# ScalarE does its part of an expert step behind the next block's first tile; the steps are dealt out anew; TensorE adds even slots' rows from slot 184

## The chip, the core and the metric

One core of a Trainium2 chip runs the whole program. The metric is the device time of one execution in microseconds (us), lower is better. The core has TensorE (PE, its weight loads are PEld), VectorE (DVE), ScalarE (ACT), GpSimd (POOL) and SyncE (SP), each with its own instruction queue; they wait for each other by semaphores, and 16 DMA engines move data for all of them. "Granted clock" is the share of full speed at which TensorE was allowed to run (1.0 is 2.4 GHz, 0.5 is 1.2 GHz).

## What is computed

Two transformer blocks over 512 positions of width 1024, all in float32. The first has chunked attention with a learned bias, a gated short convolution and a squared-ReLU feed-forward part. The second mixes stick-breaking attention and an mLSTM, and ends in a mixture of single-vector experts, which is where most bytes are read:

```python
def peer(h, w_q, sub_keys, expert_u, expert_v):
    q = einsum('bsd,dq->bsq', h, w_q)                       # 8 heads x 2 halves of 128
    scores = einsum('bshpc,hpnc->bshpn', q, sub_keys)
    top_s, top_i = lax.top_k(scores, 16)                    # per half
    cand_s, cand_i = all 256 sums and index pairs
    best_s, best_pos = lax.top_k(cand_s, 16)
    gate = softmax(best_s)                                  # 8 heads x 16 = 128 experts a token
    ...
    u = jnp.take(expert_u, ib, axis=0)                      # a row of 1024 per token and expert
    act = gelu(einsum('td,tkd->tk', xb, u))
    vv = jnp.take(expert_v, ib, axis=0)
    return einsum('tk,tkd->td', gate * act, vv)
```

## The kernel before, in words

The 512 positions are cut into two halves of 256 (`hf` 0 and 1), and each half goes through both blocks. A half is a list `SEQ` of weight **blocks**: Q1, K1, V1, CG, XC, BG, then attention with GC, CP and GA worked in between its items, then AP, WO, 16 UP, 16 DN (the feed-forward part), then for the second layer QKM, Q2, K2, V2, VM and OM (worked in between the stick-breaking heads), the mLSTM without blocks, WO2 and 8 PQ. A block is 1 MB of weights (256 columns, into a ring of four buffers by SyncE) and two **tiles** of 8 matmuls each (lines 496 and 499, two records a matmul), whose results ScalarE or VectorE take out of PSUM. There are four PSUM lanes, so TensorE can be four tiles ahead.

The experts of half 0 are worked off beside the blocks of half 1. 512 **slots** stand for them: a slot is one expert for each of 128 tokens, 128 slots to a tile of tokens. GpSimd gathers a slot's 128 rows of u and v together, 1 MB (line 449). Slots come in groups, of two up to slot 255 and of four after it. An **expert step** is the work of VectorE and ScalarE on one group, and each engine has it as a generator, `expert_steps`, which `tick` calls once after every block of half 1 but six, and the stick-breaking loop once more for every even head (`next(experts_act)`, `next(experts_dve)`). I number steps so that step k takes the dot products of group k and finishes group k-1:

- VectorE's step k: `coef` of group k-1 from ScalarE's GELU of it (line 1241, it waits for `gelu_done`), one weighted addition into `acc` for each slot (line 1256), then two dot products of group k (line 1229). Every eighth step also picks 16 more experts, the **routing** (lines 1184 to 1211).
- ScalarE's step k: it waits for VectorE's dot products of group k and does their GELU (line 888).
- From `FIRST_PE` = slot 208 on, an even slot's v row is added by TensorE instead of by VectorE: ScalarE makes a diagonal matrix of the coefficient (line 881), TensorE multiplies (line 477).

So VectorE's step k needs ScalarE's step k-1, and ScalarE's step k needs VectorE's step k. There are six gather buffers until slot 208, so up to that slot the gathers follow VectorE's pace. From 208 on (`CHANGE`, in GpSimd's list) the weight ring and other memory are free and there are 16 buffers. 100 of the steps lie beside blocks; the others follow when the last block is done.

Order is what is written: each engine's program is generated in the order of the text. Other lines that the prediction speaks of: the stick-breaking loop runs over 8 heads c. VectorE subtracts the sums (1609), adds the softplus of the next head (1597), takes in the logits of the one after (1593), and does its step at the end of the position. ScalarE does an exponential (1087), the three of `soft` for head c+2 (1077, 1079, 1081), takes out a tile of VM or OM (1094), and does its step. TensorE does logits (638), sums (648, 652), a VM or OM tile (496, 499) and values (664). In PQ, TensorE has a tile, then `side_scores` (830); ScalarE takes out the tile (1144) and the scores (1133); VectorE searches the 16 best of each score list (1690 to 1698, "top-k"). Then come transposes (850) and copies (1160), for which VectorE waits. Sums of squares for a norm are lines 912 (ScalarE) and 520 (TensorE), for heads 927 and 534.

Of the kernel before, what the change touches and what calls it, by code (L numbers as in the profile page):

```python
# [111 lines left out]

FIRST_PE = 208

# [25 lines left out]

TICKS = [int(hf == 1 and (kind, i) not in ((BG, 3), (WO, 3), (DN, 15), (V2, 0), (V2, 1), (WO2, 3))) for hf, kind, i in SEQ]
EARLY = sum(TICKS) + 4 > GROUP_OF[15 * TOPK]


def build(nc, a, out):
    ctx = ExitStack()
    with ctx:
# [314 lines left out]
        def _(pe):  # L462
# [20 lines left out]

            def weights_block(n, moving, token_major=False, first=True, last=True, fresh=None, single=False):

                pe.wait_ge(w_loaded[n % NRING], 16 * (n // NRING + 1))
                for t in range(2):
# [15 lines left out]
                    mm.then_inc(tile_done, 1)  # L503
                    if t == 0 and n:
                        for _ in range(TICKS[n - 1]):
                            next(experts_pe)
                    yield t

# [221 lines left out]
            def half(hf):  # L730
# [104 lines left out]
                for i in range(8):  # L835
                    for _ in weights_block(NO[hf, PQ, i], h, fresh=KT * (4 * hf + 3) if i == 0 else None):
                        if m:
                            side_scores(m - 1)
                        m += 1
                side_scores(15)  # L840
                pe.wait_ge(sc_done, 16 * (hf + 1))
# [29 lines left out]
        def _(act):  # L871
# [27 lines left out]
            ticked = []  # L899

            def tick(hf, kind, i):
                n = NO[hf, kind, i]
                ticked.append(n)
                for _ in range(TICKS[n]):
                    next(experts_act)

# [11 lines left out]
            def head_squares(hf, kind, m0, raw, root=None):  # L918

                for i in range(COUNT[kind]):  # L920
                    n = NO[hf, kind, i]
                    for t in range(2):
                        m = m0 + 2 * i + t
                        tile_wait(act, n, t)
                        if m >= 4:
                            act.wait_ge(ms_done, m - 3)
                        act.activation(scr[:, m % 4, :], out_tile(n, t), ACT.Square).then_inc(sq_done, 1)
                        act.activation(raw[:, 2 * i + t, :], out_tile(n, t), ACT.Copy).then_inc(evac_sem(n, t), 1)
                        if root is not None and 2 * i + t == 0:
                            head_root(hf, root)  # L930
                    tick(hf, kind, i)
# [8 lines left out]
            def evacuate(hf, kind, dst, func=ACT.Copy, root=None, **kw):  # L940

                for i in range(COUNT[kind]):
                    n = NO[hf, kind, i]
                    for t in range(2):
                        j = 2 * i + t
                        tile_wait(act, n, t)
                        extra = {k: v(j) for k, v in kw.items()}
                        act.activation(dst(i, t), out_tile(n, t), func, **extra).then_inc(evac_sem(n, t), 1)
                        if root is not None and j == 0:
                            head_root(hf, root)  # L950
# [7 lines left out]
            def attention(hf):  # L958
# [34 lines left out]

                def fill_ticks(tiles):
                    for j in tiles:
                        if j % 2:
                            tick(hf, FILL1[j // 8], j % 8 // 2)

                act.wait_ge(ms_done, 32 * hf + 16)
                exps(0)  # L1000
                for i in range(N_ITEMS + 1):
# [6 lines left out]
                    if i >= 2:  # L1008
                        prob_copy(i - 2)
                    fill_ticks(filled(i - 1))  # L1010
                prob_copy(N_ITEMS - 1)
                fill_ticks(filled(N_ITEMS))

            def half(hf):
# [17 lines left out]
                for i in range(16):  # L1032
                    n = NO[hf, UP, i]
                    for t in range(2):
# [3 lines left out]
                        evac_wait(act, n, t)  # L1038
                        act.activation(u, u, ACT.Square).then_inc(relu_sq, 1)
                    tick(hf, UP, i)  # L1040
                only_ticks(hf, DN)
# [6 lines left out]
                for j in range(8):  # L1048
# [5 lines left out]
                    if t:  # L1054
                        tick(hf, QKM, j // 2)
                tanh_half(7)
                head_squares(hf, Q2, 32 * hf + 16, QS)
# [7 lines left out]
                act.wait_ge(gate_act, 3 * hf + 2)  # L1065
                act.activation(row_a, row_a, ACT.Ln, bias=ones_1[0:NML, 0:1]).then_inc(gate_act, 1)

                _, zb, ab = sb_bufs(hf)
# [16 lines left out]
                for c in range(NH2):  # L1085
# [11 lines left out]
                    elif hf:  # L1097
                        next(experts_act)
                for j in range(4):
# [39 lines left out]
                for m in range(16):  # L1139
# [7 lines left out]
                    if t:  # L1147
                        tick(hf, PQ, m // 2)
                    if (hf, m) == (0, 7):
                        gate_exps(0)  # L1150
# [15 lines left out]
            half(1)  # L1166
            assert ticked == [n for n in range(NB) if SEQ[n][1] != ADA]
            if EARLY:
                gate_exps(16)
# [5 lines left out]
        def _(dve):  # L1175
# [161 lines left out]
            def attention(hf):  # L1337
# [39 lines left out]
                for i in range(N_ITEMS + 1):  # L1377
# [8 lines left out]
                    for j in filled(i):  # L1386
                        if j % 2:
                            tick(hf, FILL1[j // 8], j % 8 // 2)
                y_copy(7)

            def half(hf):
# [193 lines left out]

                only_ticks(hf, V2)
                dve.wait_ge(neg_done, 5 * hf + 3)
# [193 lines left out]
```

## Time and profile before

| | |
|---|---|
| median of 3 runs | 2891.6 us (2891.0 to 2894.65) |
| the profiled execution, its own time | 2893.74 us |
| its span in the profile | 2892.0 us |
| TensorE matmul, VectorE, ScalarE, GpSimd busy | 79%, 63%, 22%, 27% |
| mean granted clock | 0.888 |
| read from HBM | 790 MB, 275 GB/s over the span |

Half 0 ends and half 1 begins at 959 us. The last block ends at 2056 us; after that only the experts are left. The busy shares are means over stages with different limits, so the stages are read one by one.

### The profile page before, as it was taken

How to read it: one execution, taken by the hardware profiler on the slowest of the kernel's cores; microseconds unless marked ns; L12 is line 12 of the kernel's file. 1: busy time of each engine (PE TensorE's matmuls, PEld its weight loads, DVE VectorE, ACT ScalarE, POOL GpSimd, SP SyncE). 2: the span in 40 equal slices, each digit the busy share in tenths (PEclk: the TensorE clock that was granted, in tenths of full speed). 3: DMA queues.
4: the chain of work that ended last, by engine and by line, in shares of the span. 5: the costliest groups of instructions: out<-in, count | busy, mean ns of one | idle time of the engine just before them, and what ended most of it. 6: DMA issues, size and time to landing. Idle time of an engine off the chain costs nothing. (4 is left out here: it accounts for less than half of the span.)

```text
span 2892.0 us, 26202 instructions
## 1 busy us (share of the span) xinstructions
PE 2280.8 (79%) x9012; PEld 1681.2 (58%) x9012; DVE 1826.5 (63%) x3679; ACT 647.0 (22%) x1438; POOL 776.5 (27%) x544
## 2 busy tenths in 40 slices
PE   8999999989889998899899689987444555445554
PEld 6887788878668777677788566766311221112121
DVE  1122235413237679667777785758888888888886
ACT  1103212002611310462221115621111111111110
POOL 0000000000000244223443331312375545546552
PEclk9999999999979999899999888998677877777777
DMA  4343357643124699677899873634599999999996
GB/s 161 120 149 117 122 188 289 260 149 121 69 102 185 249 348 415 215 271 291 363 421 421 366 297 120 253 143 192 200 406 421 411 421 422 421 402 422 422 421 276
DMA packets 114660, 798.24 MB, mean 276 GB/s; under 512 B 13280, under 2 KB 16480, under 8 KB 19040
## 3 DMA queue, kind: packets, MB, share of 16 engines
q0 software_dynamic: 74880, 541.10, 46.3%
q1 hardware_dynamic: 39648, 255.47, 23.7%
q8 instruction: 72, 1.18, 0.2%
q14 instruction: 60, 0.49, 0.0%
HBM read 790.23 MB, written 6.29 MB: 275 GB/s over the span
## 5 line engine op out<-in xcount | busy, mean ns | idle before, releaser
L499 PE MATMUL PS<-reg,ring 128*128 128x256 f32 x6016 | 1381.0, 388 | 34.0 <-DVE reg L1324 13.5
L499 PEld LDWEIGHTS PS<-reg,ring 128*128 128x128 f32 x6016 | 1149.2, 194 | 221.6 <-issue 52.1
L449 POOL DMA_INDIRECT uv<-in_expert_uv,experts x322 | 519.7, 1614 | 1927.3 <-DVE experts L1211 915.1
L477 PE MATMUL PS<-uv,diag 128*128 128x512 f32 x228 | 154.2, 828 | 239.7 <-ACT diag L881 239.7
L1256 DVE SCALAR_TENSOR_TENSOR acc<-uv,coef,acc 128x1024 f32<-128x1024 f32 x261 | 335.3, 1285 | 10.3 <-DVE coef L1241 1.1
L1229 DVE CUSTOM_DVE_ANT_0 uv<-uv,h_tok 128x1024 f32<-128x1024 f32 x226 | 268.9, 1219 | 41.6 <-DMA uv<-in_expert_uv,experts 41.3
L477 PEld LDWEIGHTS PS<-uv,diag 128*128 128x128 f32 x228 | 59.1, 274 | 339.4 <-issue 339.4
L888 ACT ACTIVATE acts<-dots 128x2 f32<-128x2 f32 (+1 forms) x192 | 39.1, 204 | 944.9 <-DVE dots L1229 896.1
L477 PE MATMUL PS<-reg,diag 128*128 128x512 f32 x228 | 156.7, 840 | 103.9 <-ACT diag L881 103.9
L477 PEld LDWEIGHTS PS<-reg,diag 128*128 128x128 f32 x228 | 58.2, 270 | 200.0 <-issue 200.0
L449 POOL DMA_INDIRECT reg<-in_expert_uv,experts x114 | 141.2, 1238 | 88.7 <-PE PS L477 62.7
L1229 DVE CUSTOM_DVE_ANT_0 uv<-uv,reg 128x1024 f32<-128x1024 f32 x96 | 116.5, 1225 | 58.3 <-DMA uv<-in_expert_uv,experts 58.3
L477 PE MATMUL PS<-ring,diag 128*128 128x512 f32 x152 | 89.1, 726 | 61.9 <-ACT diag L881 61.9
L496 PE MATMUL PS<-ring,reg 128*128 128x256 f32 x512 | 117.3, 384 | 0.0
L449 POOL DMA_INDIRECT ring<-in_expert_uv,experts x76 | 106.3, 1399 | 33.6 <-issue 20.4
L1229 DVE CUSTOM_DVE_ANT_0 reg<-reg 128x1024 f32<-128x1024 f32 x96 | 112.8, 1220 | 3.4 <-DMA reg<-in_expert_uv,experts 3.4
L496 PEld LDWEIGHTS PS<-ring,reg 128*128 128x128 f32 x512 | 95.8, 191 | 18.5 <-issue 6.4
L477 PEld LDWEIGHTS PS<-ring,diag 128*128 128x128 f32 x152 | 31.8, 223 | 112.0 <-issue 112.0
L1334 DVE SCALAR_TENSOR_TENSOR reg<-reg,par,PS 128x256 f32<-128x256 f32 x64 | 28.4, 477 | 97.6 <-PE PS L552 97.6
L888 ACT ACT_TABLE_LOAD x52 | 66.7, 1283 | 98.2 <-issue 56.5
L1347 DVE SCALAR_TENSOR_TENSOR reg<-PS,toep 128x128 f32<-128x128 f32 (+1 forms) x64 | 31.2, 488 | 90.6 <-PE PS L584 86.0
L1476 DVE SCALAR_TENSOR_TENSOR tmp<-ring,silu_c,tmp 128x256 f32<-128x256 f32 x168 | 81.4, 485 | 6.0
(240 smaller groups left out, 2314.1 us busy)
## 6 DMA issues: line engine op xcount, KB each, us to landing
ring<-in_weights SPq DMA_DIRECT2D x228, 1024.0 KB, 6.8
uv<-in_expert_uv,experts POOLq DMA_INDIRECT x322
reg<-in_x_t SPq DMA_DIRECT2D x2, 1024.0 KB, 5.9
kv_half<-reg SPq DMA_DIRECT2D x1, 2048.0 KB, 10.7
reg<-in_sub_t SPq DMA_DIRECT2D x2, 1024.0 KB, 4.8
toep<-in_rel_pad SPq DMA_DIRECT2D x16, 128.0 KB, 5.1
x_tokens<-reg SPq DMA_DIRECT2D x2, 1024.0 KB, 9.1
reg<-kv_half SPq DMA_DIRECT2D x1, 2048.0 KB, 14.3
```

The lines of the kernel that those rows point to most:

```text
L449: gp.indirect_dma_start(UV[r], None, a["expert_uv_2"], bass.IndirectOffsetOnAxis(ap=experts[:, e % 256:e % 256 + 1], axis=0))\
L477: mm = pe.matmul(PS[:, 6 + j, :], diag[:, n % 4, :], UV[BUF[s]][:, D + 512 * j:D + 512 * j + 512], start=begins, stop=ends, **LAX)
L496: mm = pe.matmul(out_tile(n, t), mv[:, t * P:(t + 1) * P], w, start=first and k == 0, stop=last and k == KT - 1)
L499: mm = pe.matmul(out_tile(n, t), w[:, t * P:(t + 1) * P], mv, start=first and k == 0, stop=last and k == KT - 1)
L888: act.activation(acts[:, s0 % 16:s0 % 16 + s1 - s0], dots[:, s0 % 16:s0 % 16 + s1 - s0], ACT.Gelu)\
L1229: dve.tensor_tensor_reduce(out=u, in0=u, in1=H2[s // 256][:, s // NSLOT % 2, :], scale=1.0, scalar=0.0, op0=ALU.mult, op1=ALU.add, accum_o ...
L1256: dve.scalar_tensor_tensor(acc[:, :], v, c, acc[:, :], ALU.mult, ALU.add).then_inc(acc_done, 1)
L1334: dve.scalar_tensor_tensor(tile, tile, gain, PS[:, b, c0:c0 + T], ALU.mult, ALU.mult).then_inc(hn_done, 1)
L1347: dve.scalar_tensor_tensor(PROB[:, i % 4, 0:w], PS[:, i % 3, 0:w], HD1 ** -0.5, toep[:, hd % 2, w - 1::-1], ALU.mult, ALU.add).then_inc(s_ ...
L1476: dve.scalar_tensor_tensor(ac, ring[:, n % NRING, k, :], silu_c[:, k:k + 1], ac, ALU.mult, ALU.add)\
```

## The change

1. `ScalarE's` step is postponed. `tick` no longer does it but owes it (`owe`), and `settle` does it after the first tile of the next block has been taken out. In the list `SEQ` positions where only ticks stand, a tick settles the one before. In the stick-breaking loop `next(experts_act)` becomes `owe(1)`, and no `settle` stands inside the loop.
2. Steps are dealt out anew (`NO_STEP`, `MORE`). No step any more after BG 1, DN 11, DN 13, DN 14, QKM 1, QKM 3; new ones after V2 0 and V2 1, and three inside attention, after the first tiles of three of its blocks. That is 99 steps beside blocks where there were 100. VectorE's two V2 steps stand among the head scalings.
3. `FIRST_PE` is 184: even slots 184 to 206, 12 in all, are now TensorE's. In PQ, TensorE's part stands behind `side_scores`.

```diff
-FIRST_PE = 208
+FIRST_PE = 184
...
-TICKS = [int(hf == 1 and (kind, i) not in ((BG, 3), (WO, 3), (DN, 15), (V2, 0), (V2, 1), (WO2, 3))) for hf, kind, i in SEQ]
+NO_STEP = ((BG, 1), (BG, 3), (WO, 3), (DN, 11), (DN, 13), (DN, 14), (DN, 15), (QKM, 1), (QKM, 3), (WO2, 3))
+MORE = (2, 10, 18)
+TICKS = [int(hf == 1 and (kind, i) not in NO_STEP) for hf, kind, i in SEQ]
...
-                for _ in weights_block(NO[hf, PQ, i], h, fresh=KT * (4 * hf + 3) if i == 0 else None):
+                    n = NO[hf, PQ, i]
+                    for t in weights_block(n, h, fresh=KT * (4 * hf + 3) if i == 0 else None, steps=False):
                         if m:
                             side_scores(m - 1)
                         m += 1
+                        if t == 0:
+                            for _ in range(TICKS[n - 1]):
+                                next(experts_pe)
...
+            def settle():
+                for _ in range(owed[0]):
+                    next(experts_act)
+                owed[0] = 0
+            def owe(steps):
+                settle()
+                owed[0] = steps
             def tick(hf, kind, i):
                 n = NO[hf, kind, i]
                 ticked.append(n)
-                for _ in range(TICKS[n]):
-                    next(experts_act)
+                owe(TICKS[n])
...
                         act.activation(raw[:, 2 * i + t, :], out_tile(n, t), ACT.Copy).then_inc(evac_sem(n, t), 1)
+                        if t == 0:
+                            settle()
...
                     for j in tiles:
                         if j % 2:
                             tick(hf, FILL1[j // 8], j % 8 // 2)
+                        elif hf and j in MORE:
+                            owe(1)
+                        settle()
...
                 act.activation(row_a, row_a, ACT.Ln, bias=ones_1[0:NML, 0:1]).then_inc(gate_act, 1)
+                settle()
...
                     if t:
                         tick(hf, kind, i)
                     elif hf:
-                        next(experts_act)
+                        owe(1)
...
+                tick(hf, V2, 0)
                 for m in range(8):
                     head_scale(hf, 2, m, (QS if m < 4 else KS)[:, m % 4, :], col("q_g_2" if m < 4 else "k_g_2"))
+                    if m == 3:
+                        tick(hf, V2, 1)
...
-                only_ticks(hf, V2)
```

**The stick-breaking loop, ScalarE, half 1.** From the tile of head 0 (line 1094) on, through head 1. The 128x896 operations are one head's; `acts<-dots` is the step's GELU. Before:

```order
L1094 ACTIVATE reg<-PS 128x256
L888 ACT_TABLE_LOAD
L888 ACTIVATE acts<-dots 128x2
L1087 ACT_TABLE_LOAD
L1087 ACTIVATE reg<-reg 128x896
L1077 ACTIVATE reg<-reg 128x896
L1079 ACTIVATE reg<-reg 128x896
L1081 ACT_TABLE_LOAD
L1081 ACTIVATE reg<-reg,ones 128x896
L1094 ACTIVATE reg<-PS 128x256
L888 ACT_TABLE_LOAD
L888 ACTIVATE acts<-dots 128x2
```

After, the same place (the tile is line 1134, the GELU line 905):

```order
L1134 ACTIVATE reg<-PS 128x256
L1127 ACT_TABLE_LOAD
L1127 ACTIVATE reg<-reg 128x896
L1117 ACTIVATE reg<-reg 128x896
L1119 ACTIVATE reg<-reg 128x896
L1121 ACT_TABLE_LOAD
L1121 ACTIVATE reg<-reg,ones 128x896
L1134 ACTIVATE reg<-PS 128x256
L905 ACT_TABLE_LOAD
L905 ACTIVATE acts<-dots 128x2
```

The GELU behind head 0's tile is gone, and one stands behind head 1's tile: it is head 0's.

**The PQ blocks, half 1, late ones.** ScalarE before, from the first tile of a block (1144 a tile, 1133 scores) over its step to the next block's tile:

```order
L1144 ACTIVATE reg<-PS 128x256
L1133 ACTIVATE reg<-PS 128x2x128
L1144 ACTIVATE reg<-PS 128x256
L1133 ACTIVATE reg<-PS 128x2x128
L888 ACTIVATE acts<-dots 128x2
L1144 ACTIVATE reg<-PS 128x256
```

ScalarE after, from the first tile of a block on (1184, 1173; 898 is the diagonal, 905 the GELU):

```order
L1184 ACTIVATE reg<-PS 128x256
L1173 ACTIVATE reg<-PS 128x2x128
L898 ACTIVATE diag<-ident,coef 128x128
L905 ACTIVATE acts<-dots 128x2
L1184 ACTIVATE reg<-PS 128x256
L1173 ACTIVATE reg<-PS 128x2x128
L1184 ACTIVATE reg<-PS 128x256
```

TensorE at the same place, before and then after (830 and 843 are `side_scores`, 488 is the addition of an expert's row):

```order
L830 MATMUL PS<-reg 128x128 x2
L499 MATMUL PS<-reg,ring 128x256 x8
L830 MATMUL PS<-reg 128x128 x2
L499 MATMUL PS<-reg,ring 128x256 x8
L830 MATMUL PS<-reg 128x128 x2
```

```order
L843 MATMUL PS<-reg 128x128 x2
L488 MATMUL PS<-uv,diag 128x512 x2
L510 MATMUL PS<-reg,ring 128x256 x8
L843 MATMUL PS<-reg 128x128 x2
L510 MATMUL PS<-reg,ring 128x256 x8
L843 MATMUL PS<-reg 128x128 x2
```

The step moved from behind a block's second tile to behind the next block's first tile and scores, and TensorE has an addition ahead of each second tile from the fourth block on.

**Head scaling after V2, VectorE, half 1.** Before, from the inverse of the root on:

```order
L1329 RECIPROCAL hroot<-hroot 128x256
L1546 MEMSET reg 128x896
L1550 COPY reg<-strict 128x128 x2
L1334 SCALAR_TENSOR_TENSOR reg<-reg,par,PS 128x256 x8
L1556 TENSOR_SCALAR toep<-PS,par 4x256 x2
```

After (1377 is the scaling; 1284, 1299, 1272 are a step's coefficient, additions and dot products):

```order
L1372 RECIPROCAL hroot<-hroot 128x256
L1591 MEMSET reg 128x896
L1595 COPY reg<-strict 128x128 x2
L1284 TENSOR_TENSOR coef<-acts,gates 128x2
L1299 SCALAR_TENSOR_TENSOR acc<-uv,coef,acc 128x1024 x2
L1272 ISA uv,dots<-uv,h_tok 128x1024
L1272 ISA dots 128x1
L1272 ISA uv,dots<-uv,h_tok 128x1024
L1272 ISA dots 128x1
L1377 SCALAR_TENSOR_TENSOR reg<-reg,par,PS 128x256 x4
L1284 TENSOR_TENSOR coef<-acts,gates 128x2
L1299 SCALAR_TENSOR_TENSOR acc<-uv,coef,acc 128x1024 x2
```

Two steps stand now among the eight scalings, one before and one after the first four.

## Rows read from the trace of the kernel before

**Rows 1.** Table by stretch; the first row names its columns.

```profile
core 0: us, PE busy (x) PEld busy (x) DVE busy (x) ACT busy (x) POOL busy (x), PEclk, DMA share, GB/s
1167.00:1335.00 168.00, 160.16 (x740) 117.39 (x740) 116.35 (x230) 93.69 (x182) 44.35 (x24) 0.98 0.69 241
1407.00:1630.00 223.00, 223.00 (x1022) 195.79 (x1022) 166.85 (x266) 39.56 (x105) 88.36 (x59) 0.99 0.98 403
...
1791.00:1858.00 67.00, 66.37 (x330) 53.78 (x328) 54.44 (x74) 48.91 (x54) 26.04 (x14) 1.00 0.67 251
1954.00:2070.00 116.00, 76.72 (x320) 63.29 (x319) 97.50 (x328) 15.42 (x45) 29.43 (x16) 0.83 0.45 169
2103.00:2892.00 789.00, 395.54 (x608) 149.15 (x608) 672.14 (x1181) 123.83 (x312) 403.95 (x306) 0.75 0.98 405
```

**Rows 2.** Page: an addition. Line engine op, tiles, shapes, count | busy, mean ns | idle.

```profile
L1256 DVE SCALAR_TENSOR_TENSOR acc<-uv,coef,acc 128x1024 f32<-128x1024 f32 x261 | 335.3, 1285 | 10.3 <-DVE coef L1241 1.1
```

**Rows 3.** Timeline, TensorE after DN, half 0 and 1: start, us, what [idle before <-releaser].

```profile
642.72 3.62 PE L520 MATMUL PS<-scr,ones_d 128*128 128x256 f32 x16
...
1651.10 5.51 PE L520 MATMUL PS<-scr,ones_d 128*128 128x256 f32 x16 [20.57 <-ACT scr L912]
```

**Rows 4.** Timeline, TensorE, first head mean of Q2, half 1.

```profile
1710.33 1.12 PE L534 MATMUL PS<-scr,half_sel 128*64 128x256 f32 x2 [13.19 <-ACT scr L927]
```

**Rows 5.** Timeline, VectorE, second pair of head scalings after V2, half 1.

```profile
1756.31 0.87 DVE L1334 SCALAR_TENSOR_TENSOR reg<-reg,par,PS 128x256 f32<-128x256 f32 x2 [3.83 <-PE PS L552]
```

**Rows 6.** Timeline, all engines, one position of the stick-breaking loop.

```profile
1801.01 0.12 DVE L1241 TENSOR_TENSOR coef<-acts,gates 128x2 f32<-128x2 f32 x1
...
1805.98 1.08 DVE L1609 TENSOR_TENSOR reg<-reg,PS 128x896 f32<-128x896 f32 x1
1806.13 1.28 ACT L888 ACT_TABLE_LOAD   x1 [0.62 <-DVE dots L1229]
...
1806.98 1.08 DVE L1597 SCALAR_TENSOR_TENSOR reg<-reg 128x896 f32<-128x896 f32 x1
...
1808.39 0.70 PE L648 MATMUL PS<-reg,tri 128*128 128x256 f32 x2
...
1811.34 0.14 DVE L1241 TENSOR_TENSOR coef<-acts,gates 128x2 f32<-128x2 f32 x1
...
1811.97 3.62 PE L496 MATMUL PS<-ring,reg 128*128 128x256 f32 x16
...
1815.63 0.38 ACT L1094 ACTIVATE reg<-PS 128x256 f32<-128x256 f32 x1 [0.22 <-PE PS L496]
```

**Rows 7.** Timeline, the loop's end: a GELU without a wait, the mLSTM's start.

```profile
1847.54 1.28 ACT L888 ACT_TABLE_LOAD   x1
...
1848.83 0.20 ACT L888 ACTIVATE acts<-dots 128x2 f32<-128x2 f32 x1
...
1869.86 1.19 PE L695 MATMUL PS<-toep,ident 4*128 4x256 f32 x2 [6.08 <-DVE reg L1601]
```

**Rows 8.** Timeline, VectorE and TensorE in PQ.

```profile
2001.24 6.14 PE L499 MATMUL PS<-reg,ring 128*128 128x256 f32 x16
...
2007.31 0.14 DVE L1241 TENSOR_TENSOR coef<-acts,gates 128x2 f32<-128x2 f32 x1
...
2013.25 0.29 DVE L1690 MAX8 reg<-reg 128x8 f32<-128x128 f32 x1 [0.86 <-ACT reg L1133]
...
2020.09 0.14 DVE L1241 TENSOR_TENSOR coef<-acts,gates 128x2 f32<-128x2 f32 x1
```

**Rows 9.** Timeline, between the last block and the last stretch.

```profile
2077.44 0.16 DVE L1241 TENSOR_TENSOR coef<-acts,gates 128x2 f32<-128x2 f32 x1 [3.69 <-ACT reg L1160]
...
2082.85 0.16 DVE L1241 TENSOR_TENSOR coef<-acts,gates 128x2 f32<-128x2 f32 x1 [0.32 <-ACT acts L888]
...
2115.87 0.40 ACT L881 ACTIVATE diag<-ident,coef 128x128 f32<-128x128 f32 x1 [0.23 <-DVE coef L1241]
...
2116.42 1.95 PE L477 MATMUL PS<-uv,diag 128*128 128x512 f32 x4 [0.68 <-ACT diag L881]
```

More of the change, by code:

```diff
@@ L139, with fill_tile_no @@
     _held[_r] = _e
-TICKS = [int(hf == 1 and (kind, i) not in ((BG, 3), (WO, 3), (DN, 15), (V2, 0), (V2, 1), (WO2, 3))) for hf, kind, i in SEQ]
-EARLY = sum(TICKS) + 4 > GROUP_OF[15 * TOPK]
+NO_STEP = ((BG, 1), (BG, 3), (WO, 3), (DN, 11), (DN, 13), (DN, 14), (DN, 15), (QKM, 1), (QKM, 3), (WO2, 3))
+MORE = (2, 10, 18)
+TICKS = [int(hf == 1 and (kind, i) not in NO_STEP) for hf, kind, i in SEQ]
+STEPS = sum(TICKS) + 4 + len(MORE)
+EARLY = STEPS > GROUP_OF[15 * TOPK]
+def fill_tile_no(n, t):
+    _, kind, i = SEQ[n]
+    return 8 * FILL1.index(kind) + 2 * i + t
 def build(nc, a, out):
@@ L482, in _, with weights_block @@
             experts_pe = expert_steps()
-            def weights_block(n, moving, token_major=False, first=True, last=True, fresh=None, single=False):
+            def weights_block(n, moving, token_major=False, first=True, last=True, fresh=None, single=False, steps=True):
                 pe.wait_ge(w_loaded[n % NRING], 16 * (n // NRING + 1))
@@ L503, in weights_block @@
                     mm.then_inc(tile_done, 1)
-                    if t == 0 and n:
+                    if t == 0 and n and steps:
                         for _ in range(TICKS[n - 1]):
                             next(experts_pe)
+                    if single and SEQ[n][0] and fill_tile_no(n, t) in MORE:
+                        next(experts_pe)
                     yield t
@@ L839, in half @@
                         m += 1
+                        if t == 0:
+                            for _ in range(TICKS[n - 1]):
+                                next(experts_pe)
                 side_scores(15)
@@ L899, in _ @@
             ticked = []
+            owed = [0]
+            def settle():
[5 more added lines that the diff above has]
+                owed[0] = steps
             def tick(hf, kind, i):
@@ L992, in fill_tile, with fill_steps @@
                                        scale=0.5).then_inc(evac_sem(n, t), 1)
-                def fill_ticks(tiles):
+                def fill_steps(tiles):
                     for j in tiles:
@@ L1009, in attention @@
                         prob_copy(i - 2)
-                    fill_ticks(filled(i - 1))
+                    fill_steps(filled(i - 1))
                 prob_copy(N_ITEMS - 1)
-                fill_ticks(filled(N_ITEMS))
+                fill_steps(filled(N_ITEMS))
             def half(hf):
@@ L1039, in half @@
                         act.activation(u, u, ACT.Square).then_inc(relu_sq, 1)
+                        if t == 0:
+                            settle()
                     tick(hf, UP, i)
@@ L1055, in half @@
                         tick(hf, QKM, j // 2)
+                    else:
+                        settle()
                 tanh_half(7)
@@ L1066, in half @@
                 act.activation(row_a, row_a, ACT.Ln, bias=ones_1[0:NML, 0:1]).then_inc(gate_act, 1)
+                settle()
                 _, zb, ab = sb_bufs(hf)
@@ L1148, in half @@
                         tick(hf, PQ, m // 2)
+                    else:
+                        settle()
                     if (hf, m) == (0, 7):
@@ L1167, in _ @@
             assert ticked == [n for n in range(NB) if SEQ[n][1] != ADA]
+            settle()
             if EARLY:
@@ L1388, in attention @@
                             tick(hf, FILL1[j // 8], j % 8 // 2)
+                        elif hf and j in MORE:
+                            next(experts_dve)
                 y_copy(7)
```

1 line of the change is left out of this document (added).

## The prediction

> **What bounds the kernel now.** I read the table by stretch first, to see where a different engine ends each stage. In the last stretch (2103 to 2892) the DMA engines are 98% busy [rows 1]: it gathers slots 208 to 511, whose number the change leaves alone, so it keeps its 789 us. What the change can move is when slots 202 to 207 have been consumed, near 2103, and with it everything ahead. Ahead of that, attention and the up and down projections are TensorE's (160 of 168 us, 223 of 223). In the stick-breaking loop TensorE is busy 66 of 67 us, but VectorE and ScalarE with 54 and 49 us of it are nearly a closed loop too [rows 1]. In PQ nothing but VectorE is near full: 97.5 of 116 us [rows 1].
>
> Then the timeline, for waits that come from expert steps. After the last down projection of half 1 TensorE waits 20.57 us, where in half 0, without steps, the norm's products follow at once [rows 3]. In Q2 it waits 13.19 us for ScalarE's squares [rows 4], since ScalarE is held by GELUs of dot products not yet there. In PQ VectorE waits 0.86 us a block for scores that ScalarE brings late for the same reason [rows 8], and after the last block 3.69 us for copies [rows 9]. At the end of the stick-breaking loop a routing step holds TensorE 6.08 us [rows 7].
>
> **A step's price.** An addition is 1.29 us [rows 2]. In the loop's position a whole step (coefficients, two additions, two dot products) is 1801.01 to 1805.98, 4.97 us [rows 6]. Of the routing I take 5.5 us: most of the 6.08 us that TensorE waited for it [rows 7].
>
> **What it gives.**
> *Before attention.* VectorE is behind from CG to BG, so BG 1's missing step gives 5.0 us. Against it, ScalarE's GELU of K1 3 now stands behind V1 0's first tile, which delays a routing step that TensorE waits for, and another stands behind the wait for the stored x: I take 2.4 us. Sum -2.6 (0 to -5).
> *Attention.* Three more steps, 14.9 us of VectorE, in a stretch where it is busy 116 of 168 us and TensorE 160 [rows 1]. VectorE's own work there is about 1.4 us of a 5 us item, so a step in each of two or three items running leaves it 1.4 us behind with each, and the two routings find it a little further behind than now. +3 (0 to +15, all three exposed).
> *AP to WO.* The routing falls two blocks earlier, where VectorE can make up for it: -2 (0 to -3).
> *After DN 15.* 28 steps instead of 31 lie beside 32 blocks, and three of the last five blocks have none. The DMA engines moved 403 GB/s there at 98% [rows 1], so 32 blocks and 56 slots, 88 times 1.05 MB, need 229 us at that rate, against about 224 us of TensorE: VectorE is no longer 3.5 steps behind at the end, but may be up to 5 us. Of the 20.57 us [rows 3] I take 20 (10 to 20.57, or 22 with what the clock loses).
> *QKM to K2.* Two steps of four go from between the convolutions, but the routing now falls to the first, where ScalarE also waits for its softmax. Followed tile by tile, ScalarE's first square of Q2 comes 42.3 us after QKM begins instead of 50.0, so -8 of the 13.19 us [rows 4] (-3 to -10).
> *Scalings after V2.* Two steps of 4.97 us stand where VectorE waits 3.5 to 3.8 us ahead of each pair [rows 5]. They overrun such a hole by 1 to 2 us, but TensorE has eight matmuls of the gates between, 3.5 us, before it needs the pair. What is exposed is a table load and GELU behind the logarithm of the gates, 1.49 us, of which a wait hides part: +1 (0 to +5).
> *PQ.* Two terms. (1) ScalarE brings the scores before it waits for dot products: 0.86 us for seven blocks, 1.28 of a table load in two, and the 3.69 us of copies [rows 8, 9] are off VectorE's path, 12.3 us. (2) Six additions of 1.29 us go, 7.7 us. VectorE's block would be 12.78 (2007.31 to 2020.09) less 0.86 less 1.29, 10.6 us [rows 8]. TensorE, though, now waits for the diagonal, adds 1.95 us [rows 9], then has the second tile (3.62) and the scores: 7.4 us after the coefficients, where VectorE wants them after 7.2. So 0.3 us a block comes back, and 2 us after the routing. -16.5 (-20 to -5, the latter if TensorE stays at half clock).
> *To slot 208.* Five steps where there were four; each takes the 5.41 us of now (2077.44 to 2082.85) less one addition, 4.1 us [rows 2, 9]. 20.6 instead of 21.6; but the even slot's buffer is free only when the diagonal is made and TensorE is done (2115.87 to 2118.37, with the hand-over 2.7 us after the coefficients, where an addition was done after 1.4 us), and the gathers are late by it [rows 9]. +2 (-1 to +6).
> Sum of these: -2.6 + 3 - 2 - 20 - 8 + 1 - 16.5 + 2 = **-43.1**.
>
> **What it costs: the stick-breaking loop.** Here the late GELU has nothing that hides it. VectorE's step at position c+1 needs the GELU of position c. Before, ScalarE does it at the end of position c, as soon as the dot products are there (the load waits 0.62 us for them [rows 6]). Now it stands at the end of position c+1, behind the exponential, the three operations for a later head, and the tile. So VectorE's step, which it runs while ScalarE works, waits until ScalarE is through, and ScalarE's next exponential waits for VectorE. The loop, from the rows: step 4.97; subtraction 1.00 (1805.98 to 1806.98); softplus 1.08; TensorE's sums 3.58 (1808.39 to 1811.97); the tile, to where ScalarE takes it, 3.66 (1811.97 to 1815.63); taking it 0.38 [rows 6]; table load 1.29 and GELU 0.20 [rows 7]; 0.3 for the hand-overs. That is 16.45 us a position; it was 1801.01 to 1811.34, 10.33 [rows 6]. 6.1 us more for each of six positions (the first has its GELU, the last has neither sums nor soft): **+36.8**. The routing moves from the last position, where it was exposed, to the first, where it is exposed too: 0. And TensorE now idles about 6 us of 16.4 ahead of the sums. A tile after a wait of 4.71 us took 6.14 us instead of 3.62, at half the granted clock [rows 8]; that falls on the chain here: six times about 2 us, +12 (0 to +18). Together **+49** (37 to 58). **WO2** gets the next routing, in its first block. Three steps alone just fit beside its blocks now; with 5.5 us more VectorE comes to the last tile 3 us and ScalarE to the norm's squares 4 us later: **+4** (0 to +6).
>
> The load is priced by its row. "ScalarE: Activation LUTs" of the Trainium skill, section "What ACT_TABLE_LOAD costs", gives 2.66 us for a switch, 1.283 of load and 1.38 of drain; by it six positions would cost 8 us more. The trace shows the GELU 1.29 us behind the start of its load [rows 7], so no drain, and I go by the row.
>
> **Sum.** -43.1 + 49 + 4 = +9.9 us. On the span of 2892.0 that is 2901.9; the profiled execution was 2.1 us above the median, so on the median of 2891.6 it is **2901.5 us**.
>
> **Rivals.**
> *Full clock and full savings (0.15).* TensorE's wait in the loop doesn't lower its clock (+37), DN gives 20.6, PQ 20, attention costs nothing: -2.6 - 2 - 20.6 - 8 + 1 - 20 + 37 + 4 + 0 = -11, 2880 us. For it: each part alone is within its bounds. Against it: a wait of that length lowers the clock in every such row that I looked at. It turns to faster when the loop costs less than 33 us.
> *The late GELU is hidden (0.07).* If VectorE's step were not behind ScalarE's chain, the loop would cost nothing: -39, 2853 us. Against it stands the order of the instructions.
> *They cancel (0.18).* Loop 42 instead of 49: 2891 to 2897 us.
> *Exposed steps (0.10).* The attention steps are all exposed and PQ gains only 5: +10 + 12 + 11.5, 2925 us.
> *Forecast (0.50).* 2897.5 to 2915.
>
> **How the numbers follow.** Faster or slower by 0.2%, 5.8 us, is about what a measurement of this kernel can tell from no change. Faster 0.15 + 0.07 = 0.22, within 0.18, slower 0.50 + 0.10 = 0.60. The range holds 8 in 10: from 2878 (the hidden GELU left out, the first rival in) to 2917.
>
> **What would show it.** In the loop, VectorE's coefficients wait 5 to 7 us for the GELU, positions are 16 to 19 us apart, and TensorE's clock falls below 1.0. After DN 15 TensorE waits under 5 us instead of 20.57, in Q2 some 5 instead of 13.19. In PQ, coefficients are 10.6 to 11.2 us apart from the third block on. The last stretch stays at 789 us. If positions stay near 10.3 us, my reading of who waits for whom is wrong and the kernel is faster by some 39 us.

## The result, and the profile after

The changed kernel takes 2903.35 us (median of 6 runs, 2901.45 to 2905.3), the kernel before, timed beside it, 2893.74 us (6 runs, 2891.0 to 2894.66). The ratio is 1.0032, its 95% interval 1.0022 to 1.0042: 0.3% slower. The prediction was 2901.5 us. The profiled execution of the changed kernel took 2903.69 us with a span of 2901.7, against 2892.0 before: 9.7 us more. The sum had forecast 9.9.

Line numbers are now a little higher: coefficients 1284 (before 1241), additions 1299 (1256), GELU 905 (888), diagonal 898 (881), TensorE's addition 488 (477), weight tiles 507 and 510 (496 and 499), subtraction 1656 (1609), softplus 1644 (1597), the sums 661 (648), the exponential 1127 (1087), head mean 547 (534), the norm's products 533 (520), gathers 460 (449).

The table by stretch, changed kernel (first row: columns), answers to [rows 1]:

```profile
core 0: us, PE busy (x) PEld busy (x) DVE busy (x) ACT busy (x) POOL busy (x), PEclk, DMA share, GB/s
1166.00:1338.00 172.00, 160.91 (x741) 117.91 (x740) 130.78 (x251) 102.66 (x191) 55.74 (x30) 0.97 0.77 272
1403.00:1633.00 230.00, 226.39 (x1040) 198.70 (x1040) 168.61 (x272) 44.48 (x115) 90.40 (x58) 0.99 1.00 415
1756.00:1881.00 125.00, 86.23 (x350) 68.16 (x349) 60.20 (x91) 52.24 (x61) 26.05 (x14) 0.80 0.38 139
1972.00:2080.00 108.00, 87.16 (x376) 68.20 (x376) 92.72 (x338) 23.58 (x59) 19.54 (x15) 0.90 0.49 185
2106.00:2901.00 795.00, 395.54 (x612) 148.75 (x612) 674.68 (x1185) 124.47 (x314) 408.61 (x308) 0.75 0.98 404
```

The third row is by far the largest loss: the stick-breaking loop, which TensorE filled at full clock (66 of 67 us), has become 125 us in which no engine is full (TensorE 86, VectorE 60, ScalarE 52), at a granted clock of 0.80. Attention loses about 4 us. The gains are in the second and fourth rows: the stretch from UP to QKM is 230 us where it was 254 to the same point, and the PQ window is 108 instead of 116.

The timeline of TensorE behind the last down projection and in Q2 answers to [rows 3, 4]:

```profile
1626.20 3.62 PE L533 MATMUL PS<-scr,ones_d 128*128 128x256 f32 x16
1633.17 7.17 PE L510 MATMUL PS<-reg,ring 128*128 128x256 f32 x21 [3.35 <-DVE reg L1367]
...
1675.46 1.11 PE L547 MATMUL PS<-scr,half_sel 128*64 128x256 f32 x2 [5.12 <-ACT scr L955]
```

The norm's products (first row), which waited 20.57 us, don't wait at all, as in half 0. Q2's head mean waits 5.12 us instead of 13.19.

The stick-breaking loop in the timeline of all engines, from one step's coefficients to the next one's, answers to [rows 6]:

```profile
1797.22 0.16 DVE L1284 TENSOR_TENSOR coef<-acts,gates 128x2 f32<-128x2 f32 x1 [9.32 <-ACT acts L905]
...
1802.23 1.08 DVE L1656 TENSOR_TENSOR reg<-reg,PS 128x896 f32<-128x896 f32 x1
1803.23 1.08 DVE L1644 SCALAR_TENSOR_TENSOR reg<-reg 128x896 f32<-128x896 f32 x1
1803.35 0.95 ACT L1127 ACTIVATE reg<-reg 128x896 f32<-128x896 f32 x1 [4.86 <-DVE reg L1656]
...
1804.37 1.22 PE L661 MATMUL PS<-reg,tri 128*128 128x256 f32 x2 [5.75 <-DVE reg L1644]
...
1810.81 3.62 PE L507 MATMUL PS<-ring,reg 128*128 128x256 f32 x16
...
1814.47 0.39 ACT L1134 ACTIVATE reg<-PS 128x256 f32<-128x256 f32 x1 [4.65 <-PE PS L507]
1814.87 1.28 ACT L905 ACT_TABLE_LOAD   x1
...
1816.17 0.20 ACT L905 ACTIVATE acts<-dots 128x2 f32<-128x2 f32 x1
...
1816.40 0.16 DVE L1284 TENSOR_TENSOR coef<-acts,gates 128x2 f32<-128x2 f32 x1 [10.38 <-ACT acts L905]
```

This is the closed chain of the prediction: each engine waits for the next one in a ring, so the times add up. From the rows: step 5.01 (1797.22 to 1802.23), subtraction 1.00, softplus 1.14, sums 6.44 (1804.37 to 1810.81), tile 3.66, taking it and the GELU 1.93 (1814.47 to 1816.40), 19.18 us in all. Every engine waits in turn: VectorE 10.38 us for the GELU, ScalarE 4.86 for the subtraction and 4.65 for the tile, TensorE 5.75 for the softplus. The sums take 6.44 us where they took 3.58.

In PQ (VectorE's coefficients, and TensorE's wait for the diagonal) and between the last block and the last stretch, the timeline answers to [rows 8, 9]:

```profile
2023.35 1.96 PE L488 MATMUL PS<-uv,diag 128*128 128x512 f32 x4 [0.85 <-ACT diag L898]
...
2033.08 0.14 DVE L1284 TENSOR_TENSOR coef<-acts,gates 128x2 f32<-128x2 f32 x1
...
2043.69 0.14 DVE L1284 TENSOR_TENSOR coef<-acts,gates 128x2 f32<-128x2 f32 x1
...
2104.39 0.94 POOL L460 DMA_INDIRECT uv<-in_expert_uv,experts  x1 [4.49 <-PE PS L488]
...
2107.15 3.65 PE L488 MATMUL PS<-uv,diag 128*128 128x512 f32 x4 [3.03 <-ACT diag L898]
```

A block of PQ takes 10.61 us instead of 12.78. Behind PQ a gather waits for TensorE's addition.

### The profile page after: what moved, and what is told of

It is laid out like the page before. It is cut to its first block and busy times, and to the rows that moved or that the text cites. A ratio compares the mean times of both kernels' runs of the same rounds, so it can differ in the third digit from the quotient of the medians.

```text
span 2901.7 us, 26331 instructions
## 1 busy us (share of the span) xinstructions
PE 2306.0 (79%) x9060; PEld 1691.0 (58%) x9060; DVE 1810.6 (62%) x3667; ACT 664.9 (23%) x1459; POOL 767.9 (26%) x544
## 5 line engine op out<-in xcount | busy, mean ns | idle before, releaser
L460 POOL DMA_INDIRECT uv<-in_expert_uv,experts x322 | 512.0, 1590 | 1952.6 <-DVE experts L1254 913.6
L488 PE MATMUL PS<-uv,diag 128*128 128x512 f32 x276 | 189.3, 836 | 249.2 <-ACT diag L898 249.2
L1299 DVE SCALAR_TENSOR_TENSOR acc<-uv,coef,acc 128x1024 f32<-128x1024 f32 x249 | 319.9, 1285 | 9.4 <-DVE coef L1284 0.5
L488 PEld LDWEIGHTS PS<-uv,diag 128*128 128x128 f32 x276 | 69.8, 270 | 365.0 <-issue 365.0
L488 PE MATMUL PS<-ring,diag 128*128 128x512 f32 x152 | 83.1, 684 | 56.9 <-ACT diag L898 56.9
L1284 DVE TENSOR_TENSOR coef<-acts,gates 128x2 f32<-128x2 f32 (+1 forms) x192 | 30.5, 159 | 140.5 <-ACT acts L905 140.4
## 6 DMA issues: line engine op xcount, KB each, us to landing
kv_half<-reg SPq DMA_DIRECT2D x1, 2048.0 KB, 10.7
```

What stands on the lines that cost most here:

```text
L460: gp.indirect_dma_start(UV[r], None, a["expert_uv_2"], bass.IndirectOffsetOnAxis(ap=experts[:, e % 256:e % 256 + 1], axis=0))\
L488: mm = pe.matmul(PS[:, 6 + j, :], diag[:, n % 4, :], UV[BUF[s]][:, D + 512 * j:D + 512 * j + 512], start=begins, stop=ends, **LAX)
L1284: dve.tensor_tensor(coef[:, q:q + w], acts[:, q:q + w], gates[:, s0 % 256:s0 % 256 + w], ALU.mult)\
L1299: dve.scalar_tensor_tensor(acc[:, :], v, c, acc[:, :], ALU.mult, ALU.add).then_inc(acc_done, 1)
```

## The experiments

Each kernel was timed beside the kernel before on the same chip. For a comparison by stretch, this table gives the time in us between the starts of blocks on TensorE's timeline (the last column: from PQ to the coefficients of slots 206 and 207, on VectorE's), one profiled execution each. "Loop" is VM, OM and the mLSTM. Line numbers move by a few from kernel to kernel. The last two rows are the same program up to slot 202, and still differ by 1.7 us from UP to QKM and 3.5 us in the loop's column: a difference of that size in one stretch says nothing by itself.

| kernel | Q1 to GC | attention | AP to UP | UP to QKM | QKM to V2 | V2 to VM | loop | WO2 | PQ to 206 | median |
|---|---|---|---|---|---|---|---|---|---|---|
| before | 207.5 | 168.4 | 71.1 | 253.7 | 79.1 | 51.9 | 126.4 | 36.4 | 145.2 | 2893.7 to 2895.1 |
| changed | 208.5 | 172.3 | 65.0 | 229.7 | 70.7 | 52.0 | 174.1 | 42.0 | 134.5 | 2903.35 |
| e1_loop_at_once | 203.2 | 173.5 | 65.0 | 230.7 | 70.7 | 51.8 | 122.7 | 41.9 | 132.6 | 2852.9 |
| e2_before_loop_late | 206.8 | 168.8 | 71.2 | 253.5 | 79.4 | 51.9 | 176.9 | 36.9 | 145.6 | 2947.1 |
| e3_no_pe_rows | 208.8 | 171.4 | 65.0 | 229.7 | 71.0 | 52.2 | 174.2 | 42.0 | 138.5 | 2907.0 |
| e4_filler | 204.6 | 172.6 | 65.0 | 229.7 | 70.7 | 52.1 | 169.5 | 42.5 | 136.0 | 2900.5 |
| e5_filler_short | 207.5 | 173.1 | 65.0 | 230.7 | 70.5 | 51.8 | 168.7 | 41.1 | 132.2 | 2897.3 |
| e6_nothing_late | 203.8 | 173.2 | 65.0 | 229.7 | 71.8 | 50.9 | 124.8 | 41.2 | 146.0 | 2863.4 |
| e7_dealing_only | 203.3 | 173.6 | 65.0 | 229.8 | 71.9 | 50.9 | 128.2 | 41.2 | 150.7 | 2868.2 |
| e8_late_only | 213.8 | 168.8 | 71.2 | 256.5 | 70.3 | 51.2 | 126.4 | 36.5 | 132.7 | 2879.2 |
| e10_steps_back_to_dn | 202.9 | 164.5 | 66.2 | 250.3 | 72.5 | 51.7 | 124.7 | 41.2 | 133.8 | 2868.4 |
| e9_late_in_pq | 202.5 | 171.1 | 65.0 | 229.8 | 71.8 | 50.9 | 128.2 | 41.2 | 133.2 | 2850.4 |
| e11_no_pe_202 | 202.7 | 171.0 | 65.0 | 231.5 | 72.6 | 51.7 | 124.7 | 41.2 | 134.3 | 2849.9 |

**The loop alone, undone in the changed kernel.**

```
                     elif hf:
                         owe(1)
+                    settle()
```

> The changed kernel, with ScalarE's step in the stick-breaking loop back at the end of its own position; all else postponed as in the change. My theory: the late GELU there is the whole cost of the loop, through the closed chain and the clock that its gap lowers. Each of six positions falls from 18.2 to 19.3 us (changed kernel) to 10.3 (as before), TensorE's granted clock in the loop returns to 1.00, and the loop up to WO2 takes 174.1 less 48 = 126 us: about 2855 us, 1.3% faster than the kernel before. Rival: the loop is long because of the routing in its first position and of redistributed steps, and ScalarE's place matters for two or three positions only: less than 20 us back, 2884 or more.

Measured: 2852.9 us (2849.9 to 2861.1), ratio to before 0.9864 (0.9845 to 0.9882): 50.5 us under the changed kernel. VectorE's coefficients in the loop, and the loop as a stretch of the table:

```profile
1783.69 0.14 DVE L1285 TENSOR_TENSOR coef<-acts,gates 128x2 f32<-128x2 f32 x1
...
1794.39 0.14 DVE L1285 TENSOR_TENSOR coef<-acts,gates 128x2 f32<-128x2 f32 x1
...
1804.41 0.15 DVE L1285 TENSOR_TENSOR coef<-acts,gates 128x2 f32<-128x2 f32 x1
```
```profile
1757.00:1832.00 75.00, 70.18 (x334) 56.64 (x334) 60.17 (x93) 50.32 (x58) 26.06 (x14) 0.95 0.62 228
```

None of these coefficients waits, and these positions are 10.7 and 10.0 us. The granted clock came back to 0.95, not 1.00, and the first two positions, of which the first has the routing, still take 14.8 and 13.3 us. One line's place was worth 50 us; the rival is out.

**The loop alone, made late in the kernel before.**

```
+                late = 0
                 for c in range(NH2):
...
+                    for _ in range(late):
+                        next(experts_act)
+                    late = 0
                     if t:
-                        tick(hf, kind, i)
+                        ticked.append(n)
+                        late = TICKS[n]
                     elif hf:
-                        next(experts_act)
+                        late = 1
+                for _ in range(late):
+                    next(experts_act)
```

> The kernel before, with nothing but ScalarE's steps of the stick-breaking loop moved behind the next position's tile. My theory (the GELU there stands on a closed chain): seven positions of about 19 us instead of 10.3, with the routing at the last one: +50 to +58 us, 2942 to 2952. Rival (the cost in the changed kernel comes from the dealing out of the steps): under +10 us.

Measured: 2947.1 us, ratio 1.0179 (1.0164 to 1.0195), 52 us over before, of which the loop's column has 50.5 (126.4 to 176.9). Positions are 17.5 to 19.3 us. So the cost needs nothing of the dealing out.

**How much of it is the clock.** TensorE does products whose results the real tile overwrites, ahead of the sums, 16 of them, then 12:

```
+                    if hf and 0 < c < NH2 - 1:
...
+                        for k in range(12):
+                            pe.matmul(out_tile(n_, t_), ring[:, n_ % NRING, k % KT, t_ * P:(t_ + 1) * P],
+                                      H[:, k % KT, :], start=True, stop=True)
                     if c + 1 < NH2:
                         sums(c + 1)
```

> The changed kernel, where TensorE does 16 products more (a whole tile's, 3.6 us at full clock, whose results are overwritten by the real tile) ahead of the sums of each of six positions, in the gap of 5.8 us in which it waits for VectorE. Nothing else changes. My theory: of 8.9 us that a position is longer, 2.9 are the clock (the sums take 6.44 us instead of 3.58) and 6.1 the chain. With the gap nearly filled the clock stays at full, sums take 3.6 us and positions about 16.4 us: -15 to -18 us, 2887. Rival (the clock isn't lowered by this gap, or sums are longer for another reason, or the filler is itself in the way): 0 or up to +10 us.

> The changed kernel with TensorE's filler ahead of the sums again, but 12 products instead of 16. In the run with 16 the filler took 7.17 us (each product is two matmuls in the trace), longer than the gap, and sums began 1.1 us late: positions of 17.41 us at a clock of 1.00. 12 take 5.4 us and end inside the gap of 5.8. My theory (6.1 us of a position's 8.9 are the closed chain, 2.8 the clock): positions of 16.3 to 16.5 us, six times 1.0 us less than with 16, about 2894 us. Rival (the chain isn't closed through VectorE's step alone): positions stay above 17 us.

Measured: with 16, 2900.5 us (ratio 1.0017, 1.0007 to 1.0027); with 12, 2897.3 (1.0005, 0.9996 to 1.0014). Both missed their totals, 2887 and 2894. With 16 the filler overran the gap (7.17 us, where I had reckoned 3.6) and positions were 17.41 us. With 12, one stretch of the loop and one behind it, and VectorE's coefficients:

```profile
1811.00:1830.00 19.00, 18.63 (x89) 15.42 (x89) 10.76 (x15) 8.34 (x9) 5.79 (x4) 1.00 0.33 128
```
```profile
1869.00:1885.00 16.00, 11.97 (x30) 8.04 (x29) 10.82 (x24) 5.29 (x10) 3.84 (x2) 0.61 0.60 234
```
```profile
1809.67 0.16 DVE L1291 TENSOR_TENSOR coef<-acts,gates 128x2 f32<-128x2 f32 x1 [7.53 <-ACT acts L912]
...
1825.99 0.16 DVE L1291 TENSOR_TENSOR coef<-acts,gates 128x2 f32<-128x2 f32 x1 [8.04 <-ACT acts L912]
```

At a granted clock of 1.00 a position is 16.32 us: the closed chain by itself, against 16.45 in the prediction. In the changed kernel the five positions from 1778.97 to 1872.04 are 18.61 on average, so the clock is 2.3 us of a position. Six times that would be 14 us, but the median fell by 6 only (the profiled execution, at the lower end of its ten runs, by 10.7, of which the table's loop column has 5.4). In it the loop, from the tile of head 0 to the last coefficients, fell by 11.3 us (125.1 to 113.8), since the sixth position still took 18.00 us. From there to WO2 it took 54.9 us instead of 49.0, with a granted clock of 0.61 just behind the loop (second row) where the changed kernel has 0.76. Half of my expectation failed on this. Whether the filler is what lowered the clock behind the loop isn't shown. With 16 products that stretch took 51.7 us, so both kernels with filler are longer; but e9_late_in_pq and e11_no_pe_202, which have no filler and are the same program there, took 53.4 and 50.0 us for it, at these clocks (0.82 and 0.91):

```profile
1824.00:1877.00 53.00, 41.98 (x169) 31.53 (x167) 33.70 (x59) 17.90 (x32) 3.84 (x2) 0.82 0.20 77
```
```profile
1826.00:1876.00 50.00, 37.66 (x170) 29.04 (x168) 34.02 (x60) 17.98 (x33) 3.83 (x2) 0.91 0.21 80
```

**TensorE's rows.** `FIRST_PE` back to 208 in the changed kernel:

```
-FIRST_PE = 184
+FIRST_PE = 208
```

> The changed kernel with all additions of slots under 208 on VectorE, as before the change (no rows added by TensorE there). PQ's and the last stretch's steps have one addition of 1.29 us more for 12 even slots. By my sum six additions in PQ return 7.7 us less 2.3 of TensorE's waits for the diagonal that go, and the five steps behind PQ gain 0 to 6 us from earlier gathers against 1.29 us each: +5 us (+2 to +8), 2908. Rival (TensorE's wait for diagonals in PQ and late gathers cost as much as the additions did): 0 to -3 us.

Measured: 2907.0 us, ratio to before 1.0044 (1.003 to 1.0057), 3.7 us over the changed kernel. The intervals of the two ratios overlap, so it is the stretches that tell: from PQ to slots 206 and 207 it takes 3.9 us more (138.5 against 134.5). With additions on VectorE a block takes 11.83 us, with TensorE's rows 10.61. The pause behind those slots gives 1.9 us back (10.78 us to the next coefficients instead of 12.68).

**Nothing late; only the dealing out; only late.** The first is the changed kernel where `owe` also settles at once; the second the same with `FIRST_PE = 208`; the third is the kernel before with `owe` and `settle` everywhere but in the loop. The line that the first two have in common:

```
             def owe(steps):
                 settle()
                 owed[0] = steps
+                settle()
```

> The changed kernel with every step of ScalarE back where it was, not only those in the stick-breaking loop: the dealing out and TensorE's rows stay. Beside the run with the loop alone mended (2852.9 us) it tells what postponing is worth outside the loop. By my sum it takes 12.3 us off PQ, most of them through the scores, and costs 2.4 ahead of attention and 1 at the scalings: 2862 us (2856 to 2868). Rival (the dealing out of the steps brought all of the gain, and postponing none): 2850 to 2853.

> The kernel before with the steps dealt out anew and nothing else: no step of ScalarE is late, and TensorE adds no rows of slots under 208. By the sum: DN to QKM -22, attention to WO -2, Q2 and K2 -3 to -8, WO2 +5, and in PQ nothing: 25 to 30 us under the kernel before, 2866 us (2862 to 2872). Rival (the gain behind DN needs the late steps too): 2880 or more.

> The kernel before with ScalarE's steps postponed everywhere but in the stick-breaking loop, and nothing else: its own dealing out, no rows of slots under 208 on TensorE. By the sum: PQ and the copies behind it -12.3, ahead of attention +2.4, Q2 a few us less since the squares come ahead of the GELU: 10 us under the kernel before, 2884 us (2878 to 2889). Rival (the postponed GELU brings VectorE's coefficients as late as the scores came): 2890 to 2896.

Measured: 2863.4 us (0.988, 0.9866 to 0.9894), 2868.2 (0.9906, 0.9893 to 0.992) and 2879.2 (0.9943, 0.993 to 0.9956), each inside its own forecast. VectorE's coefficients in PQ, with only late steps and then with only TensorE's rows (nothing late):

```profile
1989.47 0.14 DVE L1284 TENSOR_TENSOR coef<-acts,gates 128x2 f32<-128x2 f32 x1
...
2001.29 0.14 DVE L1284 TENSOR_TENSOR coef<-acts,gates 128x2 f32<-128x2 f32 x1
```
```profile
1986.91 0.14 DVE L1285 TENSOR_TENSOR coef<-acts,gates 128x2 f32<-128x2 f32 x1
...
1998.32 0.14 DVE L1285 TENSOR_TENSOR coef<-acts,gates 128x2 f32<-128x2 f32 x1
```

A block of PQ is 12.78 us with neither, 11.82 late, 11.41 with the rows, 10.61 with both: the two add up (0.96 and 1.37 are 2.33, measured 2.17). Between QKM and V2 they don't: dealing out alone takes 79.1 to 71.9, late steps alone to 70.3, both together to 70.7. Either edit takes GELUs from ahead of Q2's squares, and the second finds little left: TensorE's wait at Q2's first head mean is 13.19 us before, 7.07 with the dealing alone, 4.42 with late steps alone, 5.12 with both. Late steps cost UP to QKM 2.8 us in the old dealing; in the new one all runs lie between 229.7 and 231.5, late or not.

**Late in PQ only, and the two sides of the steps' move.** `owe` settles at once until PQ of half 1. On top of this, the three steps go back from attention to DN; and, apart from that, rows 202, 204 and 206 back to VectorE.

```
                 settle()
                 owed[0] = steps
+                if not late[0]:
+                    settle()
...
+                late[0] = hf == 1
```
```
-NO_STEP = ((BG, 1), (BG, 3), (WO, 3), (DN, 11), (DN, 13), (DN, 14), (DN, 15), (QKM, 1), (QKM, 3), (WO2, 3))
-MORE = (2, 10, 18)
+NO_STEP = ((BG, 1), (BG, 3), (WO, 3), (DN, 15), (QKM, 1), (QKM, 3), (WO2, 3))
+MORE = ()
```
```
-    return s >= FIRST_PE and s % 2 == 0
+    return s >= FIRST_PE and s % 2 == 0 and not 202 <= s < 208
```

> The changed kernel, where a step of ScalarE is late in PQ only; everywhere else, ahead of attention, behind the down projections and in the stick-breaking loop too, it stands at the end of its own block. Read from the runs so far: postponing costs some 4 us ahead of attention (1160.5 against 1164 to 1171 at attention's start) and 1 us behind the down projections, gains 1 us between QKM and V2, and 12.5 us in PQ. So 3 to 4 us under the run with the loop alone mended (2852.9): 2849 us, 1.6% faster than the kernel before. Rival (the starts of attention differ from run to run for another reason): 2853.

> The kernel of the run before it in this call, with the three steps that the change put into attention back at down projections 11, 13 and 14, as before the change. It divides the two sides of that move. By the sum attention gives back 3 to 5 us and TensorE again waits some 15 us longer behind the last down projection, which VectorE reaches three steps of 5 us late: +10 us, 2859. Rival (the wait behind the last down projection went because of other edits, BG's step or the routing's place): -4 us, 2845.

> The kernel of the first run in this call, with the even slots' rows 202, 204 and 206, consumed behind the last projection, added by VectorE again; TensorE keeps slots 184 to 200. With TensorE's rows the five steps and the pause to the next took 38.8 us in the changed kernel, without them 37.8 (the run without any rows there). My theory: a gather there waits for the diagonal and TensorE, and the additions were not what bound it: 5.41 us a step, 10.8 to the next, 0 to -1 us in all. Rival: +3 x 1.29 = +4 us.

Measured: 2850.4 us (0.9854, 0.9836 to 0.9873), 2868.4 (0.9907, 0.9892 to 0.9922), 2849.9 (0.9844, 0.9825 to 0.9863). The first and the third are the fastest, 1.5% under the kernel before; 2.5 us from the run with the loop alone mended is less than these runs spread. For the second, TensorE's timeline behind the last down projection:

```profile
1637.69 5.18 PE L533 MATMUL PS<-scr,ones_d 128*128 128x256 f32 x16 [17.64 <-ACT scr L943]
...
1646.23 9.11 PE L510 MATMUL PS<-reg,ring 128*128 128x256 f32 x30 [3.35 <-DVE reg L1371]
```

The wait is back with the three steps, 17.64 us, and the products behind it take 5.18 us, not 3.62. UP to QKM grows by 20.5 us, attention shrinks by 6.6. I had put 15 against 3 to 5, the 15 as three steps of 5 us. VectorE's last steps there are longer than 5 us, since each waits for a gather; here is the second dot product of each of the last two:

```profile
1622.95 1.23 DVE L1276 CUSTOM_DVE_ANT_0 uv<-uv,h_tok 128x1024 f32<-128x1024 f32 x1 [1.96 <-DMA uv<-in_expert_uv,experts]
...
1630.41 1.22 DVE L1276 CUSTOM_DVE_ANT_0 uv<-uv,h_tok 128x1024 f32<-128x1024 f32 x1 [1.96 <-DMA uv<-in_expert_uv,experts]
```

They are 7.46 us apart, and the lower clock behind the wait comes on top. The two profiled executions differ by 21.4 us, the medians by 18.0; of the 21.4 some 4.3 stand ahead of Q1 of half 1, where the two programs don't differ: in all these runs half 1 starts between 956.8 and 962.3.

In the third, the time from the first coefficients behind PQ to the seventh is 38.41 us, and 38.43 in e9_late_in_pq, with TensorE's rows: it made no difference who adds these three rows. To the sixth it is 25.55 us with TensorE's rows and 26.59 without, and the pause to the seventh is 12.89 and 11.82: what TensorE's additions save VectorE, the later release of the buffers gives back.

## Why the prediction was right

The mechanism was the one forecast: the closed chain in the loop costs about 50 us, and one line's place switches it on and off. Of the signs, two were missed. VectorE's coefficients wait 9.3 to 11.1 us in the loop, not 5 to 7 (7.5 to 8.0 in the positions that 12 filler products held at full clock), and in PQ 10.6 us a block comes only from 2022.48 on, behind blocks of 11.83, 11.83 and 12.70.

Term by term, in the order of its sum, predicted and then measured between the profiled executions:

- **Before attention**, -2.6: +1.0 from Q1 on, and -1.6 from the spread of where half 1 starts. BG gave 6.6 as a stretch, but the price of the two late steps, 2.4, was mis-sized: V1, where the routing step stands, took 5.0 us more (33.64 to 38.66) and XC 2.4 more:

```profile
1045.21 1.69 PE L565 MATMUL PS<-hroot,spread 64*128 64x256 f32 x4 [1.74 <-DVE hroot L1372]
1046.83 6.49 PE L507 MATMUL PS<-ring,reg 128*128 128x256 f32 x16
```

  TensorE's wait is only 1.74 us; the tile behind it takes 6.49 instead of 3.72, which I counted in the loop and forgot here. In two other kernels with the same late step, e1_loop_at_once and e4_filler, the same wait left the clock up, and V1 took 35.3 us, 1.7 more than before; this is e1_loop_at_once:

```profile
1049.63 1.13 PE L565 MATMUL PS<-hroot,spread 64*128 64x256 f32 x4 [1.73 <-DVE hroot L1373]
1050.69 3.72 PE L507 MATMUL PS<-ring,reg 128*128 128x256 f32 x16
```

- **Attention**, +3: +3.9; the three steps by themselves are worth 6.6 (e10_steps_back_to_dn), so a little over half of their 14.9 us is hidden.
- **AP to WO**, -2: -6.0. The term was mis-sized: I took what VectorE makes up elsewhere, where the last WO block, from its start to UP's, went from 21.36 to 15.32 us. That its wait was VectorE's backlog with the routing in it fits the place where it went, but no run takes the routing alone.
- **After DN 15**, -20: -24.0, of which DN 15 itself is 22.6 (36.50 to 13.88). The bound had been taken as 20.57 or 22 with the clock; the upper one was right. The other 1.4 is the first UP block (10.03 to 8.67). The stretch was forecast to be held by the DMA engines at 229 us, and it measured 229.7, but that agreement is luck. TensorE's blocks stand 6.91 us apart from the second UP block to DN 15, in the kernel before and after, with no wait between; DN 15 with its norm is 13.88 and the first UP block 8.67, which adds up to 229.7. The prediction's 224 us for TensorE left out the norm. The DMA engines were 100% busy, so their limit was near, and VectorE did wait for gathers, but TensorE's only wait is the norm's own (3.35 us).
- **QKM to K2**, -8: -8.5. **Scalings**, +1: +0.2.
- **The loop**, +49: +47.6 with the mLSTM. Measured against e1_loop_at_once, the late GELU alone costs 51.4 (122.7 to 174.1), and the new dealing gives 3.7 there (126.4 to 122.7), which had been put at 0 and is about what equal programs differ by. The chain of 16.45 us a position measured 16.32 alone; the clock, taken as 2 us, was 2.3. The choice between its two levels decided the sign of the whole forecast, and the row it went by, a tile at half clock behind a wait [rows 8], was the right one: the sums took 6.44 us, not 3.58.
- **WO2**, +4: +5.5. **PQ**, -16.5: -15.2, from PQ's start to the coefficients behind its last block. **To slot 208**, +2: +4.5; five steps took 26.16 us where four had taken 21.64. A gather waits 4.49 us for TensorE's addition, the mechanism named, larger than I took it.
- **The last stretch**, 0: +2.4 (795.3 against 792.9 from the coefficients of slots 206 and 207 to the end). Its length lies between 792.6 and 798.6 us in the runs, without an order that follows the edits. What sets it stays open.

The measured terms sum to 9.8, against 9.9. The errors, +2.0 ahead of attention (+3.6 from Q1 on, less 1.6), +0.9 in attention, -4 at WO, -4 at DN, -1.4 in the loop, +1.5 at WO2, +1.3 in PQ, +2.5 and +2.4 behind it, cancelled: that the total hit by 2 us is luck, and the forecast was good to about 4 a term.

The table load went by its row: GELU starts 1.30 us behind the start of its load (1814.87 to 1816.17), and with 2.66 us, the figure of "ScalarE: Activation LUTs" of the Trainium skill, section "What ACT_TABLE_LOAD costs", the chain would by estimate have been 17.8 us at full clock. The run with 12 filler products measured 16.32, so this case's trace doesn't agree with that figure; its load alone it bears out (1.28 us).

## What to carry over

Postponing an engine's share of a side job pays where the engine has something due first (PQ: 12.5 us) and costs where the next step of another engine needs its result and the two are already in turn (the loop: 50 us). Find such a closed chain by asking of each late instruction who needs it before the engine's next own wait ends; then mend the place, not the idea. Where a change opens a gap on TensorE, price the work behind the gap at half clock as well as the gap. And when a total comes out right, look at the terms before believing them.

## What the runs showed of the hardware

The same short wait of TensorE can lower its clock or not. In V1 of half 1 it waited 1.74 us in the changed kernel, and the next tile took 6.49 us; in e1_loop_at_once it waited 1.73 us, and the same tile took 3.72.

Filling TensorE's gaps in the loop held its granted clock at 1.00 in five positions of six with 12 products, and in all six with 16 (0.80 over the loop without). Behind the loop the clock differs between kernels that have the same program there (0.82 and 0.91, 53.4 and 50.0 us), so one profiled execution doesn't tell a difference of 3 us in such a stretch.
